# Copies of old cache rows moved into two feed-forward blocks, and raw pages asked for by two engines, in a two-layer hybrid decoder step

## The reference

```python
h = h + 0.5 * swiglu(rms_norm(h, norm_ffn1[li]), w_ffn1_in[li], w_ffn1_out[li])
h = h + mix(rms_norm(h, norm_mix[li]))
h = h + 0.5 * swiglu(rms_norm(h, norm_ffn2[li]), w_ffn2_in[li], w_ffn2_out[li])
gate = sigmoid(rms_norm(h, norm_ple[li]) @ w_ple_gate[li])
h = h + gate * (p[li] @ w_ple_proj[li])
```

```python
new_win = win_all[:, -past[3].shape[1]:]          # 512 rows of 384 numbers a request
bufs.append(kv_all[:, -past[g].shape[1]:])        # dil0, dil1, dil2: 128, 512, 1024 rows of 512 numbers
```

## Time and profile before

| | |
|---|---|
| median of 3 runs | 2034.17 us |
| fastest, slowest | 2023.14, 2037.37 us |
| profiled execution, its own time | 2028.15 us |
| its span in the profile | 2026.5 us |
| mean granted TensorE clock | 0.899 of full speed |
| PE, DVE, ACT, POOL busy | 1808.3, 1059.2, 545.1, 137.1 us |

### The profile page before, as it was taken

The page is one execution under the profiler, slowest core; times in us unless marked ns, Lnnn a source line. Parts: engine busy times, 40 slices in busy tenths (PEclk is TensorE's granted clock), DMA queues, the critical chain, the costliest instruction groups (busy, mean ns, idle before and its releaser), DMA issues.

```text
span 2026.5 us, 27966 instructions
## 1 busy us (share of the span) xinstructions
PE 1808.3 (89%) x11210; PEld 1544.6 (76%) x11210; DVE 1059.2 (52%) x1513; ACT 545.1 (27%) x781; POOL 137.1 (7%) x143
## 2 busy tenths in 40 slices
PE   6999999999475998836999999999999976899998
PEld 6999966767274775414799998899997653799996
DVE  6776524535612543421467663677651653777652
ACT  5433210111001341211333422433320221443321
POOL 1000110001040110210000001100010000000010
PEclk9999989999586555866999999999999977999999
DMA  5445372218650400593334432434534515344431
GB/s 185 147 145 191 127 202 98 84 54 289 231 167 13 141 1 1 163 320 134 136 144 146 167 143 83 146 145 145 190 127 148 228 61 208 122 147 145 163 127 68
DMA packets 48239, 287.79 MB, mean 142 GB/s; under 512 B 8004, under 2 KB 17249, under 8 KB 24065
## 3 DMA queue, kind: packets, MB, share of 16 engines
q1 hardware_dynamic: 42608, 250.32, 34.2%
q0 software_dynamic: 5552, 36.41, 5.7%
HBM read 280.51 MB, written 41.62 MB: 159 GB/s over the span
## 4 chain that ended last, share of the span: by engine, by line
PE 78%; DVE 9%; DMA 4%; ACT 3%; issue 2%; SPq 1%; POOLq 1%; POOL 0%; DVEq 0%; ACTq 0%
PE ps L689 14%; PE ps L691 14%; PE ps L690 14%; PE ps L701 6%; PE ps L1340 5%; PE ps L1389 4%; DMA mem<-in_slc 3%; PE ps L2126 2%; DVE w_lo L680 2%; PE ps L1671 2%; ACT w_hi L674 2%; PE ps L1273 1%; PE ps L1547 1%; DVE mem L668 1%; PE ps L1687 1%
## 5 line engine op out<-in xcount | busy, mean ns | idle before, releaser
L689 PE MATMUL ps<-x_hi,w_hi 128*128 128x320 f32 x1408 | 439.5, 312 | 30.3 <-DVE w_lo L680 23.6
L690 PE MATMUL ps<-x_lo,w_hi 128*128 128x320 f32 x1408 | 437.8, 311 | 0.0
L691 PE MATMUL ps<-x_hi,w_lo 128*128 128x320 f32 x1408 | 437.7, 311 | 0.0
L680 DVE TENSOR_TENSOR w_lo<-live,w_hi 128x2048 fp32r<-128x2048 f32 (+1 forms) x120 | 300.6, 2505 | 180.7 <-ACT w_hi L674 180.7
L674 ACT ACTIVATE w_hi<-mem 128x2048 fp32r<-128x2048 f32 (+1 forms) x120 | 250.2, 2085 | 257.3 <-DVE mem L668 257.3
L689 PEld LDWEIGHTS ps<-x_hi,w_hi 128*128 128x128 f32 x1408 | 266.7, 189 | 35.1 <-DVE w_lo L680 26.7
L690 PEld LDWEIGHTS ps<-x_lo,w_hi 128*128 128x128 f32 x1408 | 267.0, 190 | 0.0
L691 PEld LDWEIGHTS ps<-x_hi,w_lo 128*128 128x128 f32 x1408 | 266.8, 190 | 0.0
L689 PE MATMUL ps<-act_hi,w_hi 128*128 128x320 f32 x704 | 218.4, 310 | 5.3 <-DVE w_lo L680 5.3
L690 PE MATMUL ps<-act_lo,w_hi 128*128 128x320 f32 x704 | 217.5, 309 | 0.0
L691 PE MATMUL ps<-act_hi,w_lo 128*128 128x320 f32 x704 | 217.5, 309 | 0.0
(11 more groups left out here) (383 smaller groups left out, 2068.7 us busy)
## 6 DMA issues: line engine op xcount, KB each, us to landing
live<-in_w_fi SPq DMA_DIRECT2D x88, 1024.0 KB, 4.7
live<-in_w_fo SPq DMA_DIRECT2D x32, 1408.0 KB, 5.8
mem<-in_dil SPq DMA_DIRECT2D x16, 1152.0 KB, 10.9
out_old_dil<-in_old_dil POOLq DMA_DIRECT2D x8, 2032.0 KB, 31.1
live<-in_w_even SPq DMA_DIRECT2D x12, 1024.0 KB, 4.8
mem<-in_slc SPq DMA_DIRECT2D x48, 192.0 KB, 2.9
live<-in_w_gate SPq DMA_DIRECT2D x8, 1024.0 KB, 4.8
out_old_dil<-in_old_dil SPq DMA_DIRECT2D x8, 1008.0 KB, 31.8
```

What stands on the lines that cost most here:

```text
L680: nc.vector.tensor_tensor(w_lo[:, slot, 0:w], ring[:, slot, 0:w], w_hi[:, slot, 0:w].bitcast(F32), ALU.subtract).then_inc(w_split.sem, 1)
L689: nc.tensor.matmul(out, wh, hi, start=first_k, stop=False)
L690: nc.tensor.matmul(out, wh, lo, start=False, stop=False)
L691: return nc.tensor.matmul(out, wl, hi, start=False, stop=last_k)
```

## The change

The change has two parts. The copies of old rows leave SP's queue and the end of GpSimd's work for the even mixer. GpSimd issues them inside two feed-forward blocks, one request's rows after each third chunk: `dil2` in block f=1, and `win`, `dil0` and `dil1` in block f=2. The source cuts them into rows of 8 KB (6 KB for `win`). Of each set of raw pages GpSimd asks for the even ones, and ScalarE, in a new function, for the odd ones; PE waits for both counts.

```diff
@@ sp_program, between the last even_v load and sp_save_even
-                    for name in ("win", "dil0", "dil1"):
-                        copy_old(sp, name, old_rows)
@@ act_even
             act_head_norm(act, "even", even_norm_tile)
+            act_raw(act, 0)
             act_hgrn_outputs(act)
@@ pool_raw
-            for k in range(2 * PAGES):
+            for k in range(0, 2 * PAGES, 2):
                 c = 2 * PAGES * j + k
...
+        def act_raw(act, j):
+
+            if j == 0:
+                setup_loaded.wait(act, NSETUP)
+                act.wait_ge(chunk_done.sem, first["even_o", 0])
+            elif j == 1:
+                cm_loaded.wait(act, NCM)
+            else:
+                act.wait_ge(cm_out.sem, j - 1)
+            for k in range(1, 2 * PAGES, 2):
+                c = 2 * PAGES * j + k
+                page = act.value_load(pages[0:1, c:c + 1], min_val=0, max_val=dram["cmp"].shape[0] - 1)
+                act.dma_start(raw[j % 2][:, k, :], dram["cmp"][ds(page, 1), :, :].rearrange("a p n -> (a p) n"))\
+                    .then_inc(raw_odd_loaded[j % 2].sem, 16)
@@ pe_compress
-                pe.wait_ge(raw_loaded[j % 2].sem, 16 * 2 * PAGES * (j // 2 + 1))
+                pe.wait_ge(raw_loaded[j % 2].sem, 16 * PAGES * (j // 2 + 1))
+                pe.wait_ge(raw_odd_loaded[j % 2].sem, 16 * PAGES * (j // 2 + 1))
@@ act_compress, after the two sigmoids
+            for j in range(1, NB // 2):
+                act_raw(act, j)
             act.wait_ge(cm_sum.sem, NB // 2)
...
-        def copy_old(eng, name, copied):
+        def copy_old(eng, name, b, rows):
             new = TS * (384 if name == "win" else 512)
+            eng.dma_start(out["old_" + name][b].rearrange("(k x) -> k x", k=rows),
+                          dram["old_" + name][b, new:].rearrange("(k x) -> k x", k=rows)).then_inc(old_copied.sem, 16)
+
+        def pool_copies(pool, f, copies):
             for b in range(NB):
-                eng.dma_start(out["old_" + name][b].rearrange("(k x) -> k x", k=16),
-                              dram["old_" + name][b, new:].rearrange("(k x) -> k x", k=16)).then_inc(copied.sem, 16)
+                pool.wait_ge(chunk_done.sem, first["fi", f] + 3 * b + 1)
+                for name, rows in copies:
+                    copy_old(pool, name, b, rows)
@@ pool_program
             pool_even(pool)
-            copy_old(pool, "dil2", old_last)
-            for k in range(2, 8):
+            pool_squares(pool, 2)
+            pool_copies(pool, 1, (("dil2", 254),))
+            pool_squares(pool, 3)
+            pool_squares(pool, 4)
+            pool_copies(pool, 2, (("win", 126), ("dil0", 30), ("dil1", 126)))
+            for k in range(5, 8):
                 pool_squares(pool, k)
```

More of the change, by code:

```diff
@@ L1481, in build @@
         raw_loaded = [sig(f"raw_loaded{s}", 16) for s in range(2)]
-        table_loaded = sig("table_loaded", 16)
+        raw_odd_loaded = [sig(f"raw_odd_loaded{s}", 16) for s in range(2)]
         cm_in, cm_out, cm_sum, cm_pe, cm_peb, cm_hid, cm_k, cm_v, cm_vc, cm_sq, cm_ms, cm_rt, cm_done = (
@@ L1488, in build @@
         saved = sig("saved", 16)
-        old_rows = sig("old_rows_copied", 16)
-        old_last = sig("old_last_copied", 16)
+        old_copied = sig("old_rows_copied", 16)
         def sp_save_even(sp):
@@ L2502, in sp_end @@
             sp.wait_ge(saved.sem, 8 * 16)
-            sp.wait_ge(old_rows.sem, 16 * 3 * NB)
-            sp.wait_ge(old_last.sem, 16 * NB)
+            sp.wait_ge(old_copied.sem, 16 * 4 * NB)
             sp.wait_ge(stored.sem, 4 * 16)
```

## The result

| | before | after |
|---|---|---|
| median of 4 runs | 2034.22 us | 1968.89 us |
| fastest, slowest | 2023.14, 2037.37 us | 1952.20, 1980.99 us |
| profiled execution | 2028.15 us | 1980.99 us |
| its mean granted clock | 0.899 | 0.903 |

The ratio is 0.9695, with an interval of 0.9649 to 0.9742. The forecast was 1968 us. But the profiled execution of after is the slowest of its four, and the two profiled executions lie only 2028.15 - 1980.99 = 47.2 us apart, where the sum said 62.9. So the sum has to be followed place by place.

The account below looks back on a forecast made before the run. The prediction took PE's chain as the bound, its longest non-work piece a 49.43 us page load. Gains 46.6 + 4.3 + 16 less 4 made 62.9 us, giving 1965.3 or 1971.3; forecast 1968 us, range 1950 to 1992.

Parts of the forecast that it names:

- the sum: Whole kernel: the predicted gains less the cost of copies, 46.6 + 4.3 + 16 - 4 = 62.9 us.
- The stall: Sample's last request: PE's 49.57 us wait for selected pages falls to 2.97, a gain of 46.6 us.
- The clock behind the stall: Last request's products after that wait: upper clock instead of lower, 6.63 us instead of 10.90, a gain of 4.3 us.
- its own bound of 0: Lower bound of the 4.3 us clock gain: the shorter wait already lowers the clock, so nothing is gained.
- 24 copies off SP's queue: Taking 24 copies from SP's queue ahead of the stores gains nothing.
- Raw pages by halves: Four raw-page sets: GpSimd and ScalarE each ask for half, so PE waits less; a gain of 16 us.
- The eight pages ahead of the squares: Set 0 on ScalarE: issuing eight pages delays its first squares, but PE sums them later; cost 0.
- Copies as late weights: Feed-forward blocks f=1 and f=2: copies make weight loads late, costing 4 us, with bounds 0 and 19.
- the slack of 4.8 us: Block f=1, assumed for f=2 too: a weight load may land 4.8 us late without delaying the chunk.
- The rival of 15 us more: Feed-forward blocks: copies delay weights and cost 19 us instead of 4, giving 1983 us; chance 0.13.
- the one of 96 us: Feed-forward blocks: each of 16 copies stops the weights for 6.0 us, 96 us lost, giving 2060 us; chance 0.05.
- Two bases: Starting times for the 62.9 us gain: the profiled execution gives 1965.3 us, the median of runs 1971.3.

Follow-up runs that it names:

- copies_alone: The changed kernel with all raw pages asked for by GpSimd, as in the kernel before; 1982.07 us, ratio 0.9808.
- sample_split: The changed kernel, with GpSimd instead of SP asking for every second selected page from the sample's fourth request on; 1939.31 us, ratio 0.9592.
- at_once: The changed kernel with all copies of a feed-forward block asked for together behind its first chunk; 2008.68 us in one execution.
- before_again: The kernel before, unchanged, profiled once more; 2023.06 us in one execution.
- true_rows_early: The kernel before, each `dil2` copy issued in its old place as two DMAs of every second 8 KB row; 2000.55 us, ratio 0.9841.
- after_again: The changed kernel, unchanged, run and profiled once more; 1966.28 us, ratio 0.9737.
- dil2_alone: The changed kernel with the copies of `win`, `dil0` and `dil1` back on SP where the kernel before had them; 1965.61 us in one execution.

## Why the prediction was right

- **The stall, 46.6 us: right.** 49.57 became 3.67, 45.9 us less; 3.24 in copies_alone. The wait left is a little over the 2.97 taken, because without the stall this request too meets SP's eight pages one after the other; with four of them asked for by GpSimd the same wait is 0 (sample_split).
- **The clock behind the stall, 4.3 us: the step that was wrong**, and its own bound of 0 said how: the shorter wait mostly lowers the clock as well. The request took 10.59 us after 10.90, and 9.62 to 10.71 in six of the seven profiles that lack the stall and keep SP's eight pages; only copies_alone gave the 6.63. The prediction took 859.17, where a wait of 2.97 us left the clock up, as the rule. It was one of three exceptions among the 24 waits of this size; the other two are 3.24 us in copies_alone and 3.87 in at_once, where the request took 8.03 us. Nor was 10.90 a fixed price: before_again took 8.01 behind a wait of 47.98. A little came back further on. The three profiles with a stall of 48 to 50 us all begin block f=1 with 6.8 us at the lower clock, and their blocks take 2.3 to 2.7 us more than the 448.7 of true_rows_early, which has no such stretch. Samples and blocks together took 654.7 us on average in the three profiles that keep the stall, and 611.1 in copies_alone, after and after_again. That is 43.6 us gained, where the sum had 46.6 + 4.3 - 4 = 46.9.
- **24 copies off SP's queue, nothing: right**, by dil2_alone.
- **Raw pages by halves, 16 us: right.** 67.1 to 51.2 us is 15.9, with waits of 0, 2.01 and 0.45 us where 0, 0.6 and 0 were worked out, and products that gained the clock back. The Trainium skill, "DMA: Bandwidth & Descriptors", section Issuing engines are not separate DMA queues, says that asking from several engines saves only the time of asking, usually small beside the DMA. Here it was not small: the asking was the bound, and halving it gave about 16 us in each of nine profiles with it (58.5 to 59.5 us for the stage after 75.0). The eight pages ahead of the squares cost nothing, as forecast: ACT squares first at 501.71, PE needs it at 515.78 in the first profile; where the products ran fast the stage took 56.8 us with ScalarE's pages as without (57.4 once).
- **Copies as late weights, 4 us: right in sign, a little too large.** All 32 cost 2.7 us on average, 1.5 to 5.3 in single profiles. In block f=1 the copies cost nothing that can be seen, inside the slack of 4.8 us. Block f=2 was given the same slack, and there it fell short by 1.4 to 3.8 us. The rival of 15 us more and the one of 96 us fell with it. at_once shows that the mechanism of the slower rival is real: without the spacing it takes 55 us.
- **Two bases, 1965 and 1971: needed.** Executions of one kernel differ by 29 us here (1952.20 to 1980.99) and two places of that were seen in the profiles: the clock in the prompt, 17 to 20 us, and once in the HGRN products, 10.8 us. Set against its own pair of profiles the sum looks 16 us too large, and by the second profile of after 13 us too small. The medians, 65.3 us apart in the first comparison and 58.6 in the second, lie around 62.9. That 1968 met 1968.89 is in part luck of this spread, which also covered a clock term that was too large. The sum has no term for the prompt; whether the halves make its short form more frequent, and so are worth more than their 16 us, is not shown.

## What to carry to other kernels

Copies that nothing waits for belong beside work whose loads have slack, a few at a time: one at each third chunk cost nothing, three at a time 1.4 to 3.8 us in all, and asked for all together they cost 55. Look at the built row, not the written one, since here the engines took one row of each queue in turn, so that every short row waited for a long one. And where PE waits 3 to 4 us for each small piece, count the lower clock behind the wait too: here it more than doubled the price.

## What was not expected of the hardware

- The same program got two levels of clock in the prompt: 0.50 throughout and 111.3 us in seven of 13 profiles, 91 to 94 us in four, 108.7 in two. PE was busy for 107.73 of 111 us in one of the seven, as the profile counts it, so a busy PE did not bring the clock up. All four short ones have the halves of the raw pages (four of nine with them, none of four without), which is too few to call it a cause. One execution of true_rows_early, a kernel without the halves, speaks against it: 1982.69 us at a mean granted clock of 0.914, beside 1999.39 to 2004.61 at 0.903 to 0.905. That looks like a short prompt, but there is no profile of it.
- Eight pages took ScalarE 7.65 us alone with GpSimd's eight, but 10.97 in set 0, where GpSimd's spacing grew as well, up to 2.5 us, and the DMA share was 0.90. The share alone is not the reason: before, GpSimd kept 1.14 us at nearly every page there at a share of 1.06. The cause stays open.
- `rearrange` into 254 rows changed nothing in a contiguous copy. Two DMAs of every second row did, and cost GpSimd 8.37 us of issuing instead of 3.97.
